# Input projection's first block: weights loaded in two halves, two product tiles split, row scaling inside the transposing products

## The reference

```
def rms_norm(x, g):
    x32 = x.astype(jnp.float32)
    return x32 * lax.rsqrt(jnp.mean(x32 * x32, axis=-1, keepdims=True) + EPS) * g.astype(jnp.float32)
...
    h = rms_norm(x, g).astype(x.dtype)
    p = h @ w_in
    mq, mk, mv, mo, mi, mf, dq, dk, dv = jnp.split(p, split_points(), axis=-1)
```

## Time and profile before

| | us |
|---|---|
| median of 3 runs | 689.33 |
| lowest, highest | 687.24, 695.22 |
| profiled execution | 685.39 |
| its span, first to last instruction | 683.6 |

### The profile page before, as it was taken

One profiled execution on the slowest core, in us unless ns is written; L12 is line 12 of the kernel. 1 busy time (PEld: TensorE's weight loads), 2 busy tenths in 40 slices (PEclk: granted clock), 3 DMA queues, 4 the chain that ended last, 5 costly groups with the idle time before them and its releaser, 6 DMA issues.

```text
span 683.6 us, 8735 instructions
## 1 busy us (share of the span) xinstructions
PE 621.6 (91%) x3207; PEld 336.8 (49%) x3207; DVE 285.8 (42%) x647; ACT 139.3 (20%) x409; POOL 118.6 (17%) x206
## 2 busy tenths in 40 slices
PE   4999999899999999999989996999999878999791
PEld 3444444444544565455545573655555444555440
DVE  3220058433334352669788766523212211112066
ACT  3110141333332454310131100110010000100022
POOL 2340006120040111101021201012321111120013
PEclk9999999999999999999999965999999998999996
DMA  9725247833030300043873699999999999999993
GB/s 293 224 82 176 55 164 203 274 117 124 1 109 16 123 1 1 0 124 81 238 328 134 213 392 369 352 418 421 417 400 418 421 420 420 424 417 423 416 361 129
DMA packets 59409, 165.76 MB, mean 242 GB/s; under 512 B 18345, under 2 KB 27866, under 8 KB 46694
## 3 DMA queue, kind: packets, MB, share of 16 engines
q1 hardware_dynamic: 49590, 147.97, 56.7%
q0 software_dynamic: 7552, 17.19, 7.6%
q10 hardware_dynamic: 2224, 0.04, 0.2%
HBM read 150.88 MB, written 23.34 MB: 255 GB/s over the span
## 4 chain that ended last, share of the span: by engine, by line
PE 60%; DMA 21%; DVE 6%; SPq 5%; issue 3%; ACT 3%; POOL 1%; DVEq 0%; ACTq 0%; POOLq 0%
PE bank L2015 12%; DMA WS<-in_w_down_e 9%; PE bank L2233 9%; PE bank L2012 7%; PE bank_p L2285 4%; DMA FT<-in_w_up_e 4%; PE scores L2298 3%; PE bank_t L2285 3%; SPq L581 2%; DMA WS<-out_rows 2%; PE bank_t L2029 2%; DMA MO<-in_cache_k,pages 2%; PE bank_p L2138 2%; DMA WS<-in_w_in 2%; PE scores L2155 1%
## 5 line engine op out<-in xcount | busy, mean ns | idle before, releaser
L2015 PE MATMUL bank<-WS,XHT 128*128 128x512 f32 x192 | 88.9, 610 | 2.2 <-DMA WS<-in_w_in 1.6
L2012 PE MATMUL bank<-XHT,WS 128*128 128x512 f32 x192 | 85.0, 597 | 0.6 <-PE bank_t L2029 0.6
L2015 PEld LDWEIGHTS bank<-WS,XHT 128*128 128x128 f32 x192 | 35.5, 193 | 43.7 <-issue 41.3
L2012 PEld LDWEIGHTS bank<-XHT,WS 128*128 128x128 f32 x192 | 35.7, 190 | 42.9 <-issue 42.7
L2285 PE MATMUL bank_p<-WS,XHT 128*64 128x256 f32 x288 | 45.5, 391 | 5.1 <-issue 1.7
L2285 PE MATMUL bank_t<-WS,XHT 128*64 128x256 f32 x288 | 43.0, 381 | 1.7 <-DMA FT<-in_w_up_e 1.5
L967 POOL DMA_INDIRECT out_rows<-MVA,slot_ids x15 | 15.1, 1008 | 159.7 <-DVE MVA L1825 159.7
L2285 PEld LDWEIGHTS bank_p<-WS,XHT 128*64 128x64 f32 x288 | 27.8, 141 | 19.6 <-issue 5.0
L2285 PEld LDWEIGHTS bank_t<-WS,XHT 128*64 128x64 f32 x288 | 27.2, 137 | 14.9 <-DMA FT<-in_w_up_e 2.0
L854 POOL TENSOR_SCALAR rr<-ss 128x1 f32<-128x1 f32 (+3 forms) x25 | 7.2, 287 | 150.6 <-ACT XHT L1226 43.0
L1825 DVE COPY MVA<-scores 128x512 f32<-128x512 f32 x16 | 11.1, 693 | 50.3 <-PE scores L2298 50.3
(11 more groups left out here) (473 smaller groups left out, 1052.5 us busy)
## 6 DMA issues: line engine op xcount, KB each, us to landing
WS<-in_w_gate_e SPq DMA_DIRECT2D x16, 1024.0 KB, 19.5
WS<-in_w_up_e SPq DMA_DIRECT2D x16, 1024.0 KB, 22.3
WS<-in_w_down_e SPq DMA_DIRECT2D x16, 1024.0 KB, 25.9
WS<-in_w_in SPq DMA_DIRECT2D x6, 2048.0 KB, 10.4
XHT<-in_w_gate_e SPq DMA_DIRECT2D x10, 1024.0 KB, 24.6
XHT<-in_w_up_e SPq DMA_DIRECT2D x10, 1024.0 KB, 25.9
XHT<-in_w_down_e SPq DMA_DIRECT2D x10, 1024.0 KB, 28.2
FT<-in_w_gate_e SPq DMA_DIRECT2D x6, 1024.0 KB, 23.0
```

Source lines behind the costliest of these rows:

```text
L2012: mm = pe.matmul(PS[r][:, :], w[:, k, 128 * m:128 * (m + 1)], hT[:, k, 0:512], start=(k == 0), stop=(k == KC - 1))
L2015: mm = pe.matmul(PS[r][:, :], hT[:, k, 128 * m:128 * (m + 1)], w[:, k, :], start=(k == 0), stop=(k == KC - 1))
```

## The change

The first block of weights is loaded by two transfers, k = 0 to 3 and k = 4 to 7, each with a semaphore of its own. The products of tiles 0 and 1 with block dv are split to match: both first halves are done right after the first two tiles have been turned, then the second halves at their old places in the order. Instead of scaling a tile of 128 x 1024 and transposing it, DVE now scales the 128 x 128 identity by `rr` into `scale`, and PE multiplies the unscaled tile with it: an ordinary float32 product turns and scales in one step. Two semaphores of POOL become one that counts to 2.

```diff
-    order = [("xt", 0), ("xt", 1)]
+    order = [("xt", 0), ("xt", 1), ("pre", "dv", 0), ("pre", "dv", 1)]
     for m in range(NT):
         order += [("acc", "dv", m)] + ([("xt", m + 2)] if m + 2 < NTILES else [])
...
-        hn = [HO[:, 0, :], HO[:, 1, :]]
+        scale = [HO[:, n, 0:128] for n in range(2)]
...
-                sp.dma_start(blkslot[n % 3], src).then_inc(block_in[n % 3], 16)
+                if n == 0:
+                    sp.dma_start(blkslot[0][:, 0:4], src[:, 0:4]).then_inc(head_in, 16)
+                rest = slice(4 if n == 0 else 0, KC)
+                sp.dma_start(blkslot[n % 3][:, rest], src[:, rest]).then_inc(block_in[n % 3], 16)
...
-            sp.wait_ge(dr_zeroed, 1)
+            sp.wait_ge(dr_ident_made, 1)
...
-            pool.nop().then_inc(dr_zeroed, 1)
+            pool.nop().then_inc(dr_ident_made, 1)
             link(pool.memset(ident[:, :], 0.0))
             link(pool.affine_select(out=ident[:, :], in_=ident[:, :], compare_op=ALU.not_equal, fill=1.0,
                                     base=0, pattern=[[-1, 128]], channel_multiplier=1))
-            pool.nop().then_inc(ident_made, 1)
+            pool.nop().then_inc(dr_ident_made, 1)
...
-            act.wait_ge(ident_made, 1)
+            act.wait_ge(dr_ident_made, 2)
...
                         dve.wait_ge(rsq, i + 1)
-                        v.tensor_scalar(hn[i % 2][0:n], X[0:n, i, :], rr[0:n, i:i + 1], None, ALU.mult).then_inc(hn_ready, 1)
+                        if i == 0:
+                            dve.wait_ge(dr_ident_made, 2)
+                        v.tensor_scalar(scale[i % 2][0:n, 0:n], ident[0:n, 0:n], rr[0:n, i:i + 1], None, ALU.mult)\
+                            .then_inc(hn_ready, 1)
...
+            def scaled_columns(item, j):
+
+                n = nrows(j)
+                b = banks_of(item)[0]
+                before(pe, item, b)
+                for k in range(KC):
+                    mm = pe.matmul(Sps[:, b == "Sb", 128 * k:128 * k + n], X[0:n, j, k:D:KC], scale[j % 2][0:n, 0:n],
+                                   start=True, stop=True)
+                mm.then_inc(filled[b], 1)
...
-                    if j == 0:
-                        pe.wait_ge(ident_made, 1)
                     pe.wait_ge(hn_ready, j + 1)
-                    transpose_rows(hn[j % 2], item, j)
+                    scaled_columns(item, j)
...
-                    if m == 0 and kind != "post":
+                    if m == 0 and b == "dv":
+                        pe.wait_ge(*((head_in, 16) if kind == "pre" else (block_in[0], 16)))
+                    elif m == 0 and kind != "post":
                         pe.wait_ge(block_in[n % 3], 16 * (n // 3 + 1))
```

More of the change, by code:

```diff
@@ L348, in build @@
         const_in, const_made, pad_zeroed = sem("const_in"), sem("const_made"), sem("pad_zeroed")
-        gmix_in, ident_made, dr_zeroed, wg_zeroed = sem("gmix_in"), sem("ident_made"), sem("dr_zeroed"), sem("wg_zeroed")
+        gmix_in, dr_ident_made, head_in, wg_zeroed = sem("gmix_in"), sem("dr_ident_made"), sem("block_head_in"), sem("wg_zeroed")
         gfin_in = sem("gfin_in")
```

## The result

The changed kernel is slower by 1.5%: 699.09 us median against 687.30, a ratio of 1.0148 with a 95% interval of 1.0109 to 1.0186. The forecast was +3.0 us, with a range up to 697.0 us; about +10.2 (0.0148 x 687.3) were measured. The ratio leaves out the longest run of the changed kernel, 705.75 us, which counts as slow since it lies over 1.5% above the fastest; the quotient of the two medians, with it, is 1.017.

What follows compares the result with a forecast made beforehand. Block dv's transfer, then PE almost alone up to 76.6 us, was taken to bound the front. Split and wait cancel (21.25 against 21.27), turning adds 3.0 us: 685.39 becomes 688.4; range 688.0 to 697.0 us.

Steps and rivals of the forecast that it cites:

- the price of the turning products: PE turning tiles 2, 3 and 4 by 16 product instructions each: 1.1 + 1.1 + 0.8 = +3.0 us, lower end 2.6.
- The upper end of 5.9: Turning tiles 2 to 4 if the stride's extra 0.06 us came on top each time: 2.9 us more, 5.9 in all.
- Loads that don't overlap: Rival, 0.07: strided float32 loads cannot run beside the preceding product on PE; some +24 us, over 1% from pace 0.2.
- the clock might stay low at the start: Rival, 0.15: PE's clock rises only at 18.1 us, after wide products start; sum +5.1 us, 694.4.
- The two tiles' turning: PE turning tiles 0 and 1: 32 instructions at the lower clock level, 7.9 us, from 6.95 to 14.8.
- the stretch with 64-column, load-bound products: Expert stage from 399.6 us, granted clock 0.50 with PE busy 5.12 of 5.40 us; cited for the late clock rise.
- The new wait: PE's first half of tile 1 waits for DVE's copy of turned tile 1, behind tile 2's scaling, until 17.8 us.
- the halves bring nothing by themselves: Front of PE's products with the split block dv: no gain, 21.25 against 21.27 us.
- the price of contiguous products: Turning a tile by 16 products at the pace of existing rows, 0.111 to 0.124 us each: 1.8 to 2.0 us.
- Passing on: PE's front delay reaches the end through the expert weights' issue at 344.04 us; no slack to take 3 us up.

Runs made afterwards that it cites:

- contiguous: Changed kernel with column 128k + p of the model on partition p of slice k, so turning products read weights without a stride; 687.66 us, 1.0030.
- strides: Kernel before plus overwritten series of float32 products at strides 1, 2, 3, 4, 6, 8 and transposes at 1 and 8, ahead of tile 4's turning; 751.34 us.
- Tile4_transposed: Changed kernel with tile 4 alone turned by transposes of scaled rows, tiles 0 to 3 by products; 691.34 us against 685.08, 1.0106.
- halves_only: Changed kernel with transposes of scaled rows as before; the half transfers and first-half products stay; 688.20 us, 1.0031.
- products_only: Kernel before with the turning by products alone: block dv in one transfer, no first halves; 698.34 us, 1.0182.
- halves_order: As halves_only, but DVE copies turned tile 1 before it scales tile 2; 680.04 us against 685.08, 0.9933.
- before_again: Kernel before, unedited, run for a second profile; 685.20 us, span 683.4.
- same_again: Changed kernel, unedited, run once more; 698.81 us against 686.59, 1.0158.

## Why the prediction was wrong

*The step that failed* is the price of the turning products, and in it the choice of ends: "I take the lower value, since the strided transposes keep a pace of 0.11 in spite of their longer loads". A float32 product with a strided load costs 0.23 us an instruction, not 0.11. Three tiles cost +8.55 us in place of +3.0. The transposes weren't the nearest row: a transpose keeps its pace at stride 8 (0.109 and 0.111), a float32 product takes twice as long from stride 4 on. The upper end of 5.9 was too low as well: it added the 0.06 us by which the transposes' strided loads are longer, where the product's strided load is 144 ns longer than its contiguous one (334 against 190).

*A rival named the right danger, with a mechanism that was not quite right.* "Loads that don't overlap" gave 1% from a pace of 0.2 us on and had a chance of 0.07. The pace is 0.23 and 1.5% came. But the loads aren't laid end to end with the products: with the listed 334 ns of load and a quarter of 0.43 us for the product, an instruction would take 0.44. The load's own occupancy doubled (PEld is busy for 3.9 us with tile 4's sixteen loads, for 1.9 in *contiguous*), and the product still runs beside it; hence 1.5% and not the 3.5% of that rival. *Contiguous* and *strides* show the doubling.

*The clock.* That the clock might stay low at the start was a rival; it didn't: the first half of tile 0 ran at the higher level from 14.68 us (3.60 us for eight). The two tiles' turning ended at 14.7, where 14.8 was forecast, but that is luck: the forecast had the lower level as the cause, and the pace of 0.242 us an instruction is nearly the 0.234 of a strided load at the higher one. What no term of my sum had was a fall later, behind tile 4: +1.4 to +3.0 us. The row for it stood in the prediction, the stretch with 64-column, load-bound products at a granted clock of 0.50; I used it for the start only. *Tile4_transposed* shows that it hangs on tile 4.

*The new wait* was right in place and releaser: DVE's copy of tile 1 behind tile 2's scaling, and the halves' gain lost in it. It was 1.4 us later, since tile 2's rows came at 15.5 us instead of 14.00. Over the profiles they came at 13.4 to 15.5, latest in the kernels with strided products (14.7 to 15.5) but at 14.9 without them too; with one transfer as with two. Why that is so isn't settled. That the halves bring nothing by themselves held (*halves_only*, 1.003), as did the price of contiguous products (1.78 us a tile for a forecast 1.8 to 2.0).

*Passing on.* That the front's delay reaches the end held for the large one: *products_only* has +11.6 us at block dq and +13.0 in the span of the same execution, and *halves_order* has -3.3 at block dq and -4.6 by its ratio. For small ones it didn't hold as forecast ("there is no slack in the stream to take 3 us up"): the first expert transfer is issued 3.4 us later in *before_again* than in the earlier trace rows, at 347.42 us, and the span is 0.2 us shorter; in *halves_only* it is issued at 348.93, 4.9 later, and the span is 1.1 longer. Single profiles also move by 2 us at block dq with the clock's rise.

By *halves_order*, where sixteen transposes in 3.56 us were all that PE had done before, the products behind them ran at the higher level nearly at once; in *halves_only*, behind the same transposes, they didn't. So the rule of the Trainium skill (TensorE: Matmul & The Clock Gate, Part 4, PE-mode transpose) that transposes don't count as activity that raises the clock isn't borne out by the one run and not refuted by the other.

## What to carry to other kernels

Take the price of a new instruction from a row that agrees with it in data type, mode and access pattern all at once; where no row does, measure the pair, or give the range the full distance. A float32 product with 128 moving columns or fewer took here as long as its weight load, so lay its stationary operand out contiguously (or let a transpose, which tolerates the stride, do the turning). And when a transfer is split so that work can start sooner, look for the next thing this work waits for: here three moved lines on DVE turned the same split from nothing (1.003) into a gain (0.993).

## What the hardware showed beyond that

The weight load of a float32 product has a step by stride: 0.111 and 0.118 us an instruction at strides of 1 and 2 elements, 0.171 at 3, 0.22 to 0.23 at 4, 6 and 8. Transposes showed none between strides 1 and 8, the two that were measured.

A PE that is listed as 100% busy can lose its clock. In all three profiles with strided products for tile 4, the granted clock fell to 0.50, 1.2 GHz, shortly before their end, and the sixteen wide products behind them took 8.50 to 10.03 us instead of 7.06. PE had just done sixteen load-bound instructions with 40 moving columns in some 3.96 us. Behind strided products with 128 moving columns (3.68 us for tiles 2 and 3, 5.62 us in *strides*) it didn't fall.

In all three profiles with a front some 11 us late, DVE stood still in the middle of its list at about 210 us, for 5.0 to 5.9 us, released by a queue that the trace doesn't know. From the changed kernel's chain:

```profile
210.37 0.68 DVE MO L1422
211.05 5.64 another core or an unknown queue
```

It coincides with the gathering of value pages (DMA share 0.73, 196 GB/s in 211.0 to 216.7). No profile of the other kernels has such a wait of DVE, *strides* neither, whose front was later still; so lateness alone isn't enough. What DVE waited for isn't known. In *same_again* the first expert transfer is issued at 361.33 us, 17.3 later than in the earlier trace rows, and the span is 18.2 us longer; 12.95 of that is the front, and the stall may be most of the rest. In *products_only*, which has it too, the issue is 13.5 us later for 11.6 at block dq. How much of the 10 us of the result it carries isn't known.
